# A recurrent layer's heads: the next head's queries and gate rows between a head's gates and its output products, the last head written out behind the loop

## What is computed

```
q, k, v, o, z, g = split(u @ w_in)        # per head: q, k 256 wide; v, o, z 512 wide; g: two gate scalars
logi, logf = g_i, log_sigmoid(g_f)        # rows over the 528 tokens, one for each head
s   = (q k^T) * exp(decay from logi, logf, row maximum m)    # causal
h   = (s v) / max(|sum s|, exp(-m))
h   = rmsnorm(h) * head_norm_w * sigmoid(o) * silu(z)        # "the gated output", 512 wide
out += h @ w_out[head]                                       # 1024 wide, summed over heads
x   = rmsnorm(residual + out)
```

## Time and profile before

| | us |
|---|---|
| median of 3 runs | 1727.71 (1726.42 to 1729.01) |
| the profiled execution | 1728.46 |
| its span, first to last instruction | 1726.7 |
| one head of the recurrent layer (keys to next keys, 1285.23 to 1431.9) | 146.7 |
| TensorE clock granted, mean over the span | 0.968 |

### The profile page before, as it was taken

The page is one execution under the profiler, slowest core; times in us unless marked ns, Lnnn a source line. Parts: engine busy times, 40 slices in busy tenths (PEclk is TensorE's granted clock), DMA queues, the critical chain, the costliest instruction groups (busy, mean ns, idle before and its releaser), DMA issues.

```text
span 1726.7 us, 25059 instructions
## 1 busy us (share of the span) xinstructions
PE 1636.3 (95%) x9782; PEld 1415.2 (82%) x9782; DVE 750.3 (43%) x1489; ACT 536.5 (31%) x842; POOL 606.0 (35%) x485
## 2 busy tenths in 40 slices
PE   5898999999989989999999999989999999999996
PEld 5676777777767789999999999978788778878885
DVE  5705455554565753333233321232632462262255
ACT  2332333233332343222332222232332342233232
POOL 3454212222215423344434344233243244324332
PEclk9999999999989969999999999989999999999998
DMA  8132111111113401222222222222122122112111
GB/s 330 73 115 81 50 49 49 49 49 49 49 73 116 176 25 74 96 97 90 80 83 87 97 82 89 73 74 74 49 80 76 63 73 93 53 51 95 73 49 73
DMA packets 22738, 140.56 MB, mean 81 GB/s; under 512 B 3248, under 2 KB 3248, under 8 KB 6448
## 3 DMA queue, kind: packets, MB, share of 16 engines
q1 hardware_dynamic: 18752, 131.08, 20.6%
q10 hardware_dynamic: 3952, 9.00, 1.4%
HBM read 137.98 MB, written 2.10 MB: 81 GB/s over the span
## 4 chain that ended last, share of the span: by engine, by line
issue 40%; PE 37%; POOL 17%; DVE 4%; ACT 1%; POOLq 0%; DVEq 0%; ACTq 0%
PE lin L365 31%; POOL w_lo L311 17%; PE aux L788 3%; PE aux L760 1%; DVE mix L1466 1%; PE aux L746 1%; ACT w_hi L353 0%; PE aux L442 0%; DVE squares L1484 0%; PE aux L399 0%; PE aux L716 0%; PE aux L748 0%; DVE tmp L1405 0%; DVE residual L1509 0%; ACT mix L1019 0%
## 5 line engine op out<-in xcount | busy, mean ns | idle before, releaser
L311 POOL TENSOR_TENSOR w_lo<-w_raw,w_hi 128x512 fp32r<-128x512 f32 x460 | 602.3, 1341 | 1102.2 <-ACT w_hi L353 1102.2
L365 PE MATMUL lin<-x_hi,w_hi 128*128 128x272 f32 (+1 forms) x2128 | 590.6, 331 | 24.3 <-POOL w_lo L311 17.0
L365 PE MATMUL lin<-x_lo,w_hi 128*128 128x272 f32 (+1 forms) x2128 | 579.4, 326 | 0.0
L365 PE MATMUL lin<-x_hi,w_lo 128*128 128x272 f32 (+1 forms) x2128 | 578.1, 326 | 0.0
L365 PEld LDWEIGHTS lin<-x_hi,w_hi 128*128 128x128 f32 x2128 | 358.7, 192 | 71.1 <-issue 18.2
L365 PEld LDWEIGHTS lin<-x_hi,w_lo 128*128 128x128 f32 x2128 | 358.1, 192 | 32.5
L365 PEld LDWEIGHTS lin<-x_lo,w_hi 128*128 128x128 f32 x2128 | 358.6, 192 | 28.0
L353 ACT ACTIVATE w_hi<-w_raw 128x2048 fp32r<-128x2048 f32 x115 | 219.4, 1909 | 162.1 <-PE lin L365 156.6
L860 ACT ACTIVATE prob<-prob,neg_max 128x31 f32<-128x31 f32 (+6 forms) x128 | 60.1, 471 | 157.5 <-DVE neg_max L1196 157.5
L1317 DVE TENSOR_TENSOR conv_in<-conv_c_gate,lin 128x272 f32<-128x272 f32 (+1 forms) x32 | 12.3, 427 | 213.8 <-PE lin L365 213.8
L365 PE MATMUL lin<-mix,w_hi 128*128 128x512 f32 x256 | 81.9, 401 | 10.6 <-DVE mix L1466 7.1
(11 more groups left out here) (293 smaller groups left out, 1924.4 us busy)
## 6 DMA issues: line engine op xcount, KB each, us to landing
w_raw<-wstream SPq DMA_DIRECT2D x115, 1024.0 KB, 4.8
ada_shift_scale<-w_ada SPq DMA_DIRECT2D x8, 1024.0 KB, 19.1
ada_gate<-w_ada_gate ACTq DMA_DIRECT2D x4, 1024.0 KB, 5.7
residual<-x_t SPq DMA_DIRECT2D x1, 2048.0 KB, 8.9
residual<-x_t ACTq DMA_DIRECT2D x1, 2048.0 KB, 8.4
out_t<-residual ACTq DMA_DIRECT2D x8, 256.0 KB, 2.1
small_inputs<-smalls ACTq DMA_DIRECT2D x1, 537.0 KB, 3.5
residual<-meta_t ACTq DMA_DIRECT2D x1, 64.0 KB, 11.1
```

The costliest lines, as they stand in the source:

```text
L311: ins = eng.tensor_tensor(wlo[h][:, cols], raw[h][:, cols], whi[h][:, cols].bitcast(F32), ALU.subtract)
L365: ins = t.matmul(o, w[half][:, c0:c0 + P], x(k, t0, cnt), start=(n == 0), stop=(n == 3 * kts - 1))
```

## The change

The queries chunk of head h+1 goes in front of the output weights of head h in the weight stream, and with it the spread, `head_row`, the queries' take-out, `e_m` and the decays of the next head. Head 0's queries stand ahead of the loop, the loop has three trips, and the last head is written out behind it, with no queries after its gates. The squares and their sums are formed in the last head only. The empty chunk is gone. One thing moves in every head, the last one too: ACT splits the chunk that follows the one behind chunk 7 inside the gates, between `gate_tanh(2)` and the high part of quarter 2, where before it did so behind quarter 3. In a loop head that chunk is the first half of the output weights, in the last head the second half.

```diff
 # PE
+            def head_queries(chunk, ii, head):
+                chunk_ready(START["mlstm"] + chunk, ii, 10)
+                for g in range(2):
+                    if chunk:
+                        eng.wait_ge(s_ml_out, ii * 16 + (15 + g))
+                    group(eng, chunk % 2, g * P, 256, KD, lin_outs(g, TB1), x_hi_real, x_lo_real).then_inc(s_chunk if g else s_ml, 1)
                 eng.wait_ge(s_rows, 1)
-                eng.wait_ge(s_head_row, ii + 1)
-                eng.wait_ge(s_hn_out, ii + 1)
+                eng.wait_ge(s_head_row, head + 1)
+                eng.wait_ge(s_hn_out, head + 1)
...
                 projections(range(7, 8))
+                out = 8 if last else 9
+                if not last:
+                    head_queries(8, ii, ii + 1)
...
                 for j in range(2):
-                    eng.wait_ge(s_ml_out, ii * 16 + (15 + j))
+                    eng.wait_ge(s_ml_out, ii * 16 + ((15 if last else 17) + j))
                     out_tile(j, range(3), lambda k: eng.wait_ge(s_glo, ii * 4 + (k + 1)))
 # ACT
                         for k in range(4):
                             if k >= 2:
                                 gate_tanh(k)
+                            if k == 2:
+                                chunk_lands_and_splits(eng, START["mlstm"] + 9, ii, 10)
                             eng.wait_ge(s_g, ii * 4 + (k + 1))
                             act(ghi[:, k, :], gbuf[k % 2], ACT.Copy).then_inc(s_ghi, 1)
-                chunk_lands_and_splits(eng, START["mlstm"] + 9, ii, 10)
-                for k in range(KD):
-                    if k == 4:
-                        chunk_lands_and_splits(eng, START["mlstm"] + 10, ii, 10)
...
+                if not last:
+                    head_floor(ii + 1)
+                    chunk_lands_and_splits(eng, START["mlstm"] + 10, ii, 10)
+                    head_decays(ii + 1)
+                    chunk_lands_and_splits(eng, START["mlstm"] + 11, ii, 10)
 # DVE
                 low_g(3)
+                if not last:
+                    head_row_of(ii + 1)
+                    head_queries(ii * 10 + (START["mlstm"] + 8), ii + 1)
...
                     tt(res[:, j, META:T2], res[:, j, META:T2], lin[j % 2][:, 0, :], ALU.add).then_inc(s_mlo_out, 1)
-                    norm_add_dve(eng, n4, j, T1, KD, ii)
-                own.leave(LH)
+                    if last:
+                        norm_add_dve(eng, n4, j, T1, KD)
+            head_row_of(0)
+            head_queries(START["mlstm"], 0)
+            with eng.bass.Fori(0, LH - 1, 1, engines=[eng.engine]) as ii:
+                own.enter(ii, 15)
+                head(ii, False)
+                own.leave(LH - 1)
+            head(LH - 1, True)
```

More of the change, by code:

```diff
@@ L721, in _, with head_projections @@
             norm_spread_pe(eng, n3, TB2)
[L723 to L740, removed]
+            def head_projections(ii, chunks, after_first=None):
+                for c in chunks:
+                    chunk_ready(START["mlstm"] + c, ii, 10)
+                    for g in range(2):
+                        j = 2 * c + g
+                        eng.wait_ge(s_ml_out, ii * 16 + (j - 1))
+                        if c == 1:
+                            eng.wait_ge(s_mlo_out, ii * 8 + (g - 1 + CREDIT))
+                        if j < 8:
+                            ins = group(eng, c % 2, g * P, 256, KD, lin_outs(g, TB2), x_hi, x_lo)
+                        else:
+                            ins = group(eng, c % 2, g * P, 256, KD, lin_outs(g, TB1), x_hi_real, x_lo_real)
+                        ins.then_inc(s_chunk if g else s_ml, 1)
+                        if g == 0 and after_first:
+                            after_first()
@@ L750, in _, with head, projections @@
                 ins.then_inc(s_bc, 1)
+            def head(ii, last):
+                def projections(chunks, after_first=None):
+                    head_projections(ii, chunks, after_first)
                 projections(range(1, 3))
@@ L965, in _, with head_decays, head_floor, head @@
             act(row[2], row[2], ACT.Ln, bias=1.0).then_inc(s_rows_act, 1)
[L967 removed]
+            def head_decays(head):
+                eng.wait_ge(s_masked, head + 1)
+                for j, (s0, ln, t0) in enumerate(KBLOCKS):
+                    past = t0 + P if j else 0
+                    if past < T1:
+                        ins = act(att[0:ln, j, past:T1], neg_m[0:ln, past:T1], ACT.Exp, bias=ucur[0:ln, j:j + 1])
+                    if j:
+                        ins = act(att[0:ln, j, t0:past], att[0:ln, j, t0:past], ACT.Exp, bias=ucur[0:ln, j:j + 1])
+                ins.then_inc(s_decay, 1)
+            def head_floor(head):
+                eng.wait_ge(s_bc, head + 1)
+                act(e_m[:], aux[1][:], ACT.Exp, scale=-1.0).then_inc(s_bc_act, 1)
+            def head(ii, last):
                 def output_gate_tanh(c):
@@ L1387, in _, with head_row_of, head_queries, head @@
             eng.sem_inc(s_hn_out, 1)
[L1389 to L1392, removed]
+            def head_row_of(head):
+                ts(head_row[0:LH, :], ones[0:LH, :], ident[0:LH, bass.ds(head, 1)], None, ALU.mult).then_inc(s_head_row, 1)
+            def head_queries(first, head):
+                for g in range(2):
+                    if g:
+                        eng.wait_ge(s_chunk, first + 1)
+                    else:
+                        eng.wait_ge(s_ml, head * 8 + 1)
+                    tt(qk[:, g, 0:T1], u_rstd[:, META:T2], lin[g][:, 0, :], ALU.mult).then_inc(s_ml_out, 1)
+                eng.wait_ge(s_bc, head + 1)
+                copy(neg_m[:], aux[0][:])
+                ln = STILES[0][1]
+                copy(ucur[0:ln, 0:1], aux[3][0:ln, U_COL:U_COL + 1])
+                copy(ucur[:, 1:], aux[3][:, U_COL + 1:U_COL + NST]).then_inc(s_bc_dve, 1)
+                eng.wait_ge(s_bc_dve, head + 1)
+                for j, (s0, ln, t0) in enumerate(KBLOCKS):
+                    if j:
+                        ins = tt(att[:, j, t0:t0 + P], neg_m[:, t0:t0 + P], mask[:], ALU.add)
+                ins.then_inc(s_masked, 1)
+            def head(ii, last):
                 own.up(ts(hcur[:], head_c[:, bass.ds(ii * 4, 4)], 0.25, None, ALU.mult))
```

71 lines of the change are left out of this document (30 added, 41 removed).

## The result

| | median us (range, runs) | ratio to before, 95% interval |
|---|---|---|
| before | 1727.68 (1726.07 to 1729.21, 20) | |
| changed | 1731.97 (1728.89 to 2290.15, 20) | 1.0023 (1.0016 to 1.003) |
| changed, measured again on another occasion | 1734.31 (1731.51 to 1737.69, 6), before 1727.84 | 1.0042 (1.003 to 1.0054) |

The change costs 4 to 6 us; 1725.4 was forecast, and the range ended at 1728.6.

What follows compares the result with a forecast made beforehand. PE was taken as the bound, busy for 1636.3 of 1726.7 us. Loop heads -6.0, last head +3.3 and clock +0.4 gave -2.3 us on the 1727.71 median: 1725.4 us, range 1721.8 to 1728.6.

Steps and rivals of the forecast that it cites:

- The other things that moved have cover: Loop heads: the later weight splits finish before PE wants them, and SP's loads keep their rhythm; no time was added.
- The five rivals: Five alternative outcomes set beside the forecast's own case, with chances 0.13, 0.15, 0.05, 0.07 and 0.10; own case 0.50.
- I let these stand: Behind the spreads of heads 1 to 3: clock falls of 3.4 us, costing 1.7 us each, were taken as unchanged.
- rival 2: Loop heads: the clock doesn't fall behind one or two spreads, each sparing 1.7 us; 1723.7 or 1722.0; chance 0.15.
- the hole: Loop heads: PE's wait among the first output products gets filled by queries, 2.0 us a head, 6.0 us in three.
- rival 4: Loop heads: PE still stands for the hole's time, ahead of the spread, awaiting `head_row`; 1731.1, half of it 1728; chance 0.07.
- the last head: Last head's gates: the moved split has no cover, 3.3 us lost to late low parts, plus 0.4 for the clock.
- Rival 1: Last head: little is lost, 0.4 to 1 us, as DVE wins against POOL or ACT's order doesn't hurt; 1722.4; chance 0.13.
- rival 5: Last head: each of four DVE operations waits for a full piece of POOL, losing 5.3 us; 1727.4; chance 0.10.
- Rival 3: Last head: two waits bring the clock to 0.50 for 13.7 us, costing 6.8 instead of 0.4; 1731.8; chance 0.05.
- both of the forecast's cases: Last head: the clock halves after the first wait, costing 0.5 us, or after the second, up to 1.7; 0.4 was added.

Runs made afterwards that it cites:

- e1: The changed kernel measured again with nothing further altered, for an undisturbed profile: 1734.31 us, ratio 1.0042 to before.
- e6: The kernel before with 27 extra one-column matmuls on PE ahead of the head loop: 1734.21 us, ratio 1.0036 to before.
- e2: The changed kernel with 16 extra one-column matmuls on PE between head 0's queries and its spread: 1722.26 us, ratio 0.9969 to before.
- e5: The changed kernel with both e2's 16 extra matmuls and e3's later split in the last head: 1719.29 us, ratio 0.9959 to before.
- e7: The changed kernel with all four heads written out, no hardware loop and no extra matmuls: 1724.3 us, ratio 0.9979 to before.
- e8: The changed kernel with all heads written out and e3's later split in the last head: 1719.32 us, ratio 0.9956 to before.
- e9: e2 with POOL held back, in the last chunk only, until the last quarter's low part is done: 1719.98 us, ratio 0.9954 to before.
- e10: e2 run again unaltered, as partner to e9: 1720.03 us, ratio 0.9965 to before.
- e4: The kernel before with only ACT's moved split, in all four heads: 1741.37 us, ratio 1.0078 to before.
- e3: The changed kernel with the last head's ACT split moved back behind the last quarter: 1730.01 us, ratio 1.0013 to before.

## Why the prediction was wrong, point by point

**The step that failed** is "The other things that moved have cover". It followed weights, splits, DVE and SP, each with the work that hides it, and left out the one thing that moved with them: PE's own code. Writing out head 0's queries ahead of the loop pushes the loop's body some 125 instructions down, and the body, kept over four trips before, is fetched on every trip. In its place the runs showed 2.5 us at each of two jumps (+5.1, e1), in e6 the same on the kernel before, and nothing in e2, e5, e7, e8, e9 and e10. The five rivals all weighed waits, POOL and the clock; none was about code, so the range had no room for it.

**The clock.** "I let these stand", of the falls behind the spreads, held in e1 only as a sum. Each stand at a jump brought a fall of its own in e1, 1.7 us each. Behind the spreads the fall isn't fixed: in e1 it was missing in the first loop head and double in the third, three times 3.4 us as before, so rival 2's gain didn't come there; its ground, that there is one fall or none, doesn't hold against the double one. In other executions it did come: e2 has falls at 1260.8 and 1404.1 alone, e5 and e10 none before the last head.

**Right: the hole.** 2.0 us were forecast for a loop head and the filled place is in the trace. The head's period without a fall is 143.1 us (e5); before it is 146.7 with one fall of 1.7, so 145.0: 1.9 us gained. `head_row` was never waited for behind the gates (rival 4 is out; its 1731.1 should have been 1731.4 by the forecast's own terms, 3.7 us for the last head), the old 0.8 us at the first query tile stayed at 0.74, and queries and spread took 11.3 and 3.0 us as worked out.

**Right: the last head.** Forecast were 3.3 + 0.4 us. PE's last stretch grew by 3.0 (e1, 28.9 us against 25.9) to 4.2 (e2 and e10, 30.1); in e4 the price was 3.4 a head. In e1 and in e10 PE comes to the end of its second wait equally late, 10.44 us behind chunk 7's last matmul against 7.55 before: 2.9 us for the forecast's 3.3. The rest is the clock, and both of the forecast's cases came about. In e1 it fell between the waits, where it cost nothing that shows, since the second wait shrank to 0.5 us; in e10 it fell behind the second, for 1.3. The price of DVE beside POOL, 1.3 to 1.8 us an operation, is near that in the earlier trace rows (1.52 to 1.78), the last one comes to 1.0 as POOL's end caps it, and e9 shows that all of it goes when POOL waits. Rival 1 (a loss of 0.4 to 1) and rival 5 (5.3) are out. Rival 3, slower by a long fall of the clock, is out as well: the last head's fall is 3.4 us long, not 13.7. That the sign came out as this rival had it was for another reason.

**The sum** with what was measured in e1: -6.0 for the holes, +5.1 for the jumps, +3.4 for the clock and +3.0 for the last head are +5.5 us, between the +4.3 and +6.5 of the two measurements. The profiled execution itself was only 3.1 longer: its four rows give -0.7, +1.8, +3.0 and -1.0. The forecast had -6.0 and +3.7 of the sum, so it lacked the 5.1 and the 3.4, and these 3.4 are the two falls behind the stands, the same omission.

**Open:** why the clock falls behind one spread and not behind the next, and how many blocks of code PE holds. That the number of borders decides is concluded, not shown, though the first trip's packets agree (6, 7, 6, 7 in before, e1, e2, e6). With 256 instructions to a packet, as the spacing in the trace has it, a body of 1576 is 6.16 packets long and crosses six borders from most places and seven from 40 in 256. Counted from before's place, the bodies of before and e2 (189 later: 125 and 64 of fillers) lay outside such a stretch and those of e6 (108, as 27 fillers are 108 rows) and e1 (125) inside it, which agrees.

## What to carry to other kernels

When a change writes code out ahead of a hardware loop or lengthens its body, look at the packets of instructions by trip and at waits for "issue" at the jump; a body that was kept may now be fetched on every trip, and sixteen one-column matmuls, or the loop written out, can be worth more than the reordering. And a gain that is the same for every trip but the last should be split from the last trip's loss: here ACT's split belonged late in the last head (with that and no stands, e5 and e8 took 0.996 of before, where the change as made gave 1.002 to 1.004). Whether it had to be early in the loop heads no run tried.

## What was unexpected in the hardware

**The loop's code.** A body of 1576 instructions ran four trips on 7 packets (one of them ahead of the loop), with no further fetch; moved by 108 instructions (e6) or 125 (e1), it cost 2.5 us at each jump, with four packets in a burst (e1). Written out (e7), the same work was fetched in passing at no cost. The Trainium skill says in "Runtime: NRT & Kernel Launch", section "Instruction fetch mechanics", that code comes in blocks of 16 KiB, that PE has room for 128 KiB, and that a taken branch out of the current window of two pages forces a fetch and a stall. The blocks and the stall agree with the packets of e1 and its 2.5 us; the window of two does not, since before jumped back over six borders three times without a packet. By that page's room an estimate is eight blocks: a body that crosses seven borders would fill all eight. No run here measured the room by itself.

**A stand costs more than its length.** At or just behind six of the seven jump stands of e1, e3 and e6 the granted clock went to 0.50 for 3.4 us, another 1.7 us each, though PE was idle for only 2.2 to 2.6 us and busy on both sides.
